# Layer 0's output projection, norm and queries: tile 0 first, tiles 1 to 4 beside its expert pass

## The chip, the cores and the metric

One core of a Trainium2 chip runs the whole program in one launch. The metric is the device time of that launch in microseconds. TensorE (PE) multiplies, VectorE (DVE), ScalarE (ACT) and GpSimd (POOL) work on elements, SyncE (SP) issues transfers, and 16 DMA engines move the bytes. GpSimd issues the indirect transfers (gathers). All data is float32.

## The reference

A two-layer transformer trunk, width 1024, over 512 prompt tokens and 64 sample tokens. In the kernel these are five tiles of 128 rows: 0 to 3 the prompt, 4 the sample (64 rows used). Layer 0 mixes tokens with MLA attention (`o_a`, 512 columns) and an RWKV-7 recurrence (`o_b`, 512 columns); layer 1 with two other mixers. Behind each mixer comes an expert network ("peer"), which picks for every token and each of 8 heads 16 of the rows of two tables:

```python
x = x + jnp.concatenate([o_a, o_b], axis=-1) @ w_out          # even_layer
...
x = x + peer_ffn(rmsnorm(x, norm_ffn), p_wq, p_keys, p_u, p_v)  # run_trunk
...
q = (xb @ w_q).reshape(PEER_BLOCK, PEER_HEADS, 2, half)        # peer_ffn
sc = jnp.einsum('thpd,hpnd->thpn', q, keys)
s1, i1 = lax.top_k(sc[:, :, 0], PEER_TOPK)
s2, i2 = lax.top_k(sc[:, :, 1], PEER_TOPK)
...
top_s, top_pos = lax.top_k(cand, PEER_TOPK)
gate = jax.nn.softmax(top_s, axis=-1)
ue = u_tab[eidx]
ve = v_tab[eidx]
h = jax.nn.gelu(jnp.einsum('td,thkd->thk', xb, ue))
return jnp.einsum('thk,thkd->td', gate * h, ve)
```

## The kernel before

It has stages that follow each other, each a block of its own in which all engines start and end together: norm and input projection of layer 0, `mla`, `rwkv` (two blocks), `project_out`, `norm` with the block `tail`. What the change touches begins at the end of `rwkv`.

`project_out` (L696) fetches the output weights WO as four pieces of 1024 KB (L693) and all X rows again (L147, L148), since X was scratch space in `rwkv`. For each of the five tiles it transposes the attention half OC (L725), copies it to OT, makes two groups of eight products of 128x512 (L738; the RWKV half OBT needs no transpose) and adds them to X on VectorE (L768). `norm` then squares the rows on ScalarE (L184), takes means (L203), the power -0.5 on GpSimd, scales to XN (L210), transposes (L226) and copies to XT (L190), for all five tiles.

The block in `tail` (L2200) makes the expert queries of all tiles first: for each of 8 heads eight products of 512 columns and eight of 64 (L2322), each group copied to QP by ScalarE. `pe_route` multiplies the queries of one tile and head by the keys (L1328), ScalarE copies the scores (L1336), and `dve_route` (from L1355) picks the 16 experts in some 18 steps; its first call runs alone, later ones a step or two at a time between the rows. The first group is routed behind head 0 of the queries, the second behind head 1, yet its scores are copied by ScalarE behind all heads.

The passes run over (layer, tile) in the order 0, 1, 4, 2, 3 in each layer. A pass has 8 heads (4 for tile 4) of 16 slots, 1152 slots in all. In slot s:
- GpSimd gathers, for each of 128 tokens, one row of 8 KB (u and v of the expert, L1434) into place s % 8 of `ring`; it waits until slot s - 8 is used up.
- VectorE makes the dot product of the u half with XN (L1445), ScalarE the gelu and the weight (L1475, L1480).
- TensorE adds the weighted v half in PSUM, by a diagonal that ScalarE builds (L1490) and two products of 128x512 (L1505). In slots that `on_vector` names VectorE does this instead, with one instruction on X (L1455): the first three slots of a pass, and every third, second or fourth slot in the stretches of `SHARES` (L1287).

Layer 1's mixers run beside the slots. A `Layer1` object holds a list of turns for each engine, each with a slot number; `Beside.until` gives an engine's turns when its loop over the slots has come there. The order on an engine is so fixed in the code, and a turn that waits holds up what is behind it. Weights come in slabs of at most 1024 KB, two places in turn, by SP's queue. The first mixer's turns begin at slot 324, the second's at 580; SP runs ahead, and loads the first mixer's gain and first two slabs as soon as the queries are copied.

## Time and profile before

| what | us |
|---|---|
| median of three runs | 3987.99 |
| the three runs | 3987.38, 3987.99, 3992.89 |
| the profiled execution | 3992.78 |
| its span, first to last instruction | 3991.0 |

The rows further down come from the profiled execution. L12 is line 12 of the kernel before. A timeline row gives its start and its length in us, then the engine, the line, the operation, what it writes and reads, and in brackets how long the engine was idle before and what ended that. Of a group of pipelined products the ends are modelled. PEclk is the TensorE clock granted, as a share of full speed. Where a row says SPq, the sequencer of SP issues a transfer.

### The profile page before, as it was taken

To read this page: it belongs to the slowest core of one execution; us is meant where nothing else is said; L and a number is where in the kernel's file an instruction comes from. 1 tells how busy PE (TensorE), PEld (TensorE's weight loads), DVE (VectorE), ACT (ScalarE), POOL (GpSimd) and SP (SyncE) were. 2 spreads that over 40 slices of the span, in tenths; PEclk is the share of its full clock that TensorE was granted. 3 is DMA by queue.
4 is the path that set the end of the run, shared out by engine and by line. 5 is a ranking of instruction groups with operands and counts; after the bars stand their busy time and mean duration, and the time that the engine had idled before them with its cause. 6 is when DMAs were issued, how large, how long until landed. Compare 5 with 4: busy or idle time off the path is not lost.

```text
span 3991.0 us, 34096 instructions
## 1 busy us (share of the span) xinstructions
PE 3176.5 (80%) x9530; PEld 1540.5 (39%) x9530; DVE 2664.8 (67%) x6438; ACT 1344.4 (34%) x3975; POOL 1388.1 (35%) x1218
## 2 busy tenths in 40 slices
PE   7866499787777777779898987888898887776777
PEld 4444389543222332224343442333343422332232
DVE  0087655225667666677999767689977767667664
ACT  1144222012333333333367333333553323333332
POOL 0021000012434444344543444444344444444443
PEclk9987599799999999999999999999899999999999
DMA  3100000237999999999999999999999999999998
GB/s 128 36 1 6 0 1 1 70 122 277 421 421 421 421 418 408 422 404 419 405 384 340 418 386 421 418 420 412 344 417 421 421 402 422 421 421 419 414 416 356
DMA packets 211406, 1284.78 MB, mean 322 GB/s; under 512 B 23568, under 2 KB 38928, under 8 KB 63632
## 3 DMA queue, kind: packets, MB, share of 16 engines
q0 software_dynamic: 165888, 1208.03, 73.9%
q1 hardware_dynamic: 45328, 74.57, 5.3%
q8 instruction: 76, 1.25, 0.1%
q14 instruction: 114, 0.93, 0.1%
HBM read 1278.12 MB, written 3.87 MB: 321 GB/s over the span
## 4 chain that ended last, share of the span: by engine, by line
DMA 37%; PE 20%; DVE 10%; issue 7%; ACT 3%; POOL 2%; DVEq 0%; ACTq 0%; POOLq 0%; SPq 0%
DMA ring<-in_uv,route 36%; PE banks L1505 15%; DVE ring L1445 4%; PE banks L2322 2%; POOL ring L1434 1%; DVE X L1455 1%; ACT route L1490 1%; PE banks L1893 1%; DVE own L2141 1%; ACT route L1475 1%; ACT route L1480 1%; PE banks L1859 0%; PE banks L1833 0%; DMA own<-in_l_peer_wq 0%; DVE QP L2142 0%
## 5 line engine op out<-in xcount | busy, mean ns | idle before, releaser
L1505 PE MATMUL banks<-ring,route 128*128 128x512 f32 (+1 forms) x4224 | 2032.1, 618 | 585.5 <-ACT route L1490 562.4
L1445 DVE SCALAR_TENSOR_TENSOR ring<-ring,XN 128x1024 f32<-128x1024 f32 x1152 | 1409.5, 1224 | 747.7 <-DMA ring<-in_uv,route 739.0
L1434 POOL DMA_INDIRECT ring<-in_uv,route x1152 | 1289.0, 1119 | 1747.0 <-PE banks L1505 1561.9
L1505 PEld LDWEIGHTS banks<-ring,route 128*128 128x128 f32 (+1 forms) x4224 | 745.7, 187 | 1716.4 <-issue 877.3
L1475 ACT ACTIVATE route<-route 128x2 f32<-128x2 f32 x576 | 117.2, 204 | 1837.5 <-DVE ring L1445 1837.1
L1490 ACT ACTIVATE route<-IDN,route 128x128 f32<-128x128 f32 x928 | 318.8, 386 | 1.0 <-PE banks L1505 0.4
L1480 ACT ACTIVATE route<-route 128x1 f32<-128x1 f32 x1152 | 276.7, 287 | 23.2
L1833 PE MATMUL banks<-own,QP 128*128 128x512 f32 (+1 forms) x400 | 177.2, 567 | 4.5 <-DMA own<-in_l_w_in 2.3
L111 POOL TENSOR_TENSOR ys<-ys,IDN 128x4 f32<-128x4 f32 x9 | 9.1, 1008 | 388.6 <-DVE ys L1188 388.6
L1475 ACT ACT_TABLE_LOAD x106 | 136.0, 1283 | 1.9
L1455 DVE SCALAR_TENSOR_TENSOR X<-ring,route,X 128x1024 f32<-128x1024 f32 x96 | 123.0, 1282 | 0.9
L414 PE MATMUL banks<-XT,W 128*128 128x512 f32 (+1 forms) x448 | 121.3, 433 | 0.0
L1833 PEld LDWEIGHTS banks<-own,QP 128*128 128x128 f32 x400 | 76.8, 193 | 93.4 <-issue 82.6
L1445 DVE DVE_READ_ACCUMULATOR ring<-ring,XN 128x1 f32 x1152 | 95.2, 83 | 0.0
L1342 ACT ACT_TABLE_LOAD x72 | 92.4, 1283 | 1.3
L441 DVE COPY SH<-PB 128x14 f32<-128x14 f32 x1 | 0.2, 174 | 137.9 <-ACT PB L430 137.9
L414 PEld LDWEIGHTS banks<-XT,W 128*128 128x128 f32 x448 | 67.7, 191 | 53.9 <-issue 53.9
L1048 PE MATMUL banks<-chunk_more 128*128 128x128 f32 x576 | 78.0, 288 | 12.7 <-DVE chunk_more L1175 4.9
L1048 PEld LDWEIGHTS banks<-chunk_more 128*128 128x128 f32 x576 | 71.6, 200 | 15.9 <-DVE chunk_more L1175 5.8
L1885 PE MATMUL banks<-own,QP 128*128 128x512 f32 x160 | 75.1, 594 | 1.3 <-DMA own<-in_l_w_out 1.2
L1893 PE MATMUL banks<-own 128*128 128x320 f32 (+1 forms) x256 | 71.9, 421 | 5.2 <-DMA own<-in_l_peer_wq 5.2
L1355 DVE MAX8 route<-route 128x8 f32<-128x128 f32 x144 | 34.6, 282 | 55.8 <-ACT route L1336 43.3
(411 smaller groups left out, 3348.3 us busy)
## 6 DMA issues: line engine op xcount, KB each, us to landing
ring<-in_uv,route POOLq DMA_INDIRECT x1152
own<-in_l_w_in SPq DMA_DIRECT2D x16, 1024.0 KB, 16.0
own<-in_l_peer_wq SPq DMA_DIRECT2D x9, 1024.0 KB, 15.9
own<-in_l_w_out SPq DMA_DIRECT2D x8, 1024.0 KB, 16.4
W<-in_l_w_in SPq DMA_DIRECT2D x2, 2560.0 KB, 21.7
X<-in_x_prompt SPq DMA_DIRECT2D x8, 512.0 KB, 8.5
WO<-in_l_w_out SPq DMA_DIRECT2D x4, 1024.0 KB, 9.0
own<-in_l_w_in SPq DMA_DIRECT2D x4, 656.0 KB, 15.8
```

Source lines behind the costliest of these rows:

```text
L414: m = pe.matmul(bank[n % 4][:, 0:b - a], W[:, k, ACOLS + f * P:ACOLS + (f + 1) * P], XT[:, k, a:b], start=(k == 0), stop=(k == KD - 1))
L1048: m = pe.matmul(b[:, p * n:(p + 1) * n], lhs[:, p, :], rhs[:, p, :], start=True, stop=True)
L1342: act.activation(self.GX, self.BS, ACT.Exp, bias=self.NM, accum_out=self.GS[:, 0:1]).then_inc(self.exped.h, 1)
L1434: pool.indirect_dma_start(self.ring[:, s % RING, :], None, self.io[f"uv{of_slot(s)[0]}"], bass.IndirectOffsetOnAxis(ap=self.EI[:, g % 2, k ...
L1445: dve.scalar_tensor_tensor(u, u, 1.0, self.XN[:, of_slot(s)[1], :], ALU.mult, ALU.mult, accum_out=self.HD[:, g % 2, k:k + 1]).then_inc(sel ...
L1455: dve.scalar_tensor_tensor(x, self.ring[:, s % RING, D:], self.WG[:, g % 2, k:k + 1], x, ALU.mult, ALU.add).then_inc(self.v_vector.h, 1)
L1475: act.activation(self.HG[:, par, k:k + 2], self.HD[:, par, k:k + 2], ACT.Gelu).then_inc(self.gelus.h, 1)
L1480: act.activation(self.WG[:, par, k + i:k + i + 1], self.HG[:, par, k + i:k + i + 1], ACT.Copy, scale=self.GT[:, g % 3, k + i:k + i + 1]).t ...
L1490: act.activation(self.DG[:, n % 4, 0:cols], on, ACT.Copy, scale=self.WG[:, par, k + i:k + i + 1]).then_inc(self.diagonals.h, 1)
L1505: m = pe.matmul(self.bank[1 + half][0:n, :], self.DG[:, (V_TENSOR[s] - 1) % 4, 0:n], self.ring[:, s % RING, D + 512 * half:D + 512 * half ...
L1833: m = pe.matmul(out[:, 0:W.shape[2]], self.QP[:, self.tiles[i], k, :], W[:, k % HK, :], start=(k == 0), stop=(k == KD - 1))
L1893: m = pe.matmul(out[:, 0:self.width()], W[:, k % HK, i * P:i * P + P], self.XQ[:, k, 0:self.width()], start=(k == 0), stop=(k == KD - 1))
```

## The change

`project_out`, `norm` for layer 0's experts and their queries are split by tile. The block of `tail` now does output projection, norm and all eight heads of queries for tile 0 alone. A new class `Layer0` does them for tiles 1 to 4 by turns beside the slots of the first pass, as `Layer1` does: output products from slot 9 (one product in 0.71 slots), the norms from slot 48.5, queries from slot 66 to 106. Its weights are fetched a second time, in eight slabs. WO for tile 0 is fetched during the last chunk of `rwkv`, into `ring`; for that `ring` and `own` are allocated from the start, and the stages before use them as scratch in place of buffers of their own. The first six steps of the second group's routing are done ahead of the first dot product. `SHARES` gets the entry (6, 108, 3). VectorE waits for all X rows and the small tables before its first routing, SP loads layer 1's first slabs when `Layer0`'s queries are done.

```diff
-SHARES = [(334, 404, 3), (492, 537, 2), (590, 650, 4), (770, 802, 4), (816, 848, 4)]
+SHARES = [(6, 108, 3), (334, 404, 3), (492, 537, 2), (590, 650, 4), (770, 802, 4), (816, 848, 4)]
...
                 sp.dma_start(ST[:, :, :], io["wkv_t"]).then_inc(loaded.h, 16)
+                wv = io["l0_w_out"].rearrange("(k p) n -> p k n", p=P)
+                for i in (1, 0):
+                    k = slice(4 * i, 4 * i + 4)
+                    sp.dma_start(first_out[:, k, :], wv[:, k, :]).then_inc(wl[i].h, 16)
...
+class Layer0:
...
+        for i in range(4):
+            pe.append((out - 6 + i, "out_turn", i))
+            act.append((out - 4.4 + i, "out_turn", i))
+            for j in range(NO):
+                n = 4 * j + i
+                for k in range(HK):
+                    pe.append((out + (n + k / HK) * o, "out", j // 2, i, HK * (j % 2) + k))
+                if j % 2:
+                    dve.append((out + (n + 1) * o + 1.8, "add", j // 2, i))
+            x = norm + step * i
+            act.append((x, "square", i))
+            dve.append((x + 1, "mean", i))
+            pool.append((x + 1, "root", i))
+            dve.append((x + 3, "scale", i))
+            for b in range(2):
+                pe.append((x + 4 + b, "turn", i, b))
+                act.append((x + 5.6 + b, "xt", i, b))
+        for j in range(NQ):
+            for i in range(4):
+                n = 4 * j + i
+                for k in range(HK):
+                    pe.append((query + (n + k / HK) * q, "query", j // 2, i, HK * (j % 2) + k))
+                if j % 2:
+                    act.append((query + (n + 1) * q + 1.8, "query", 4 * (j // 2) + i))
+        dve.append((query, "zero"))
...
+        for s in range(NO + NQ):
+            if s >= 2:
+                self.slab_end(sp, s - 2)
+            w, c = (w_out, s) if s < NO else (w_q, s - NO)
+            sp.dma_start(self.W[s % 2], w[:, HK * (s % 2):HK * (s % 2) + HK, 512 * (c // 2):512 * (c // 2) + 512]
+                         ).then_inc((self.sl0, self.sl1)[s % 2].h, 16)
...
+            m = pe.matmul(out[:, 0:3 * P + DEC], W[:, k % HK, i * P:i * P + P], self.XQ[:, k, 0:3 * P + DEC],
+                          start=(k == 0), stop=(k == KD - 1))
...
+            sp.dma_start(X[:, 0, :], io["x_prompt"][0, 0:P, :]).then_inc(xl.h, 16)
+            sp.dma_start(rest.GM, io["l0_norm_ffn"].partition_broadcast(P)).then_inc(gl.h, 16)
+            sp.dma_start(WQ, io["l0_peer_wq"].rearrange("(k p) n -> p k n", p=P)).then_inc(wq.h, 16)
             sp.wait_ge(kz.h, kz.at(1))
...
+            for t in range(1, 4):
+                sp.dma_start(X[:, t, :], io["x_prompt"][0, t * P:(t + 1) * P, :]).then_inc(ol.h, 16)
+            sp.dma_start(X[0:DEC, 4, :], io["x_sample"][0]).then_inc(ol.h, 16)
...
-            sp.wait_ge(ev.h, ev.at(QUERIES))
+            rest.sp(sp)
             one.sp(sp)
...
+            for b in range(2):
+                for n, k in enumerate((4, 5, 6, 7, 0, 1, 2, 3)):
+                    if b == 0 and n % 4 == 0:
+                        pe.wait_ge(wo[k // 4].h, wo[k // 4].at(16))
+                    if b == 0 and n == 4:
+                        pe.wait_ge(ot.h, ot.at(1))
+                    lhs = QP[:, 0, k, :] if k < 4 else OBT[:, k - 4, 0:P]
+                    m = pe.matmul(bank[4 + b], lhs, WO[:, k, b * 512:(b + 1) * 512], start=(n == 0), stop=(n == KD - 1))
+                m.then_inc(mm_.h, 1)
...
             for h in range(PH):
...
+                for k in range(KD):
+                    m = pe.matmul(bank[3 + h % 4][:, 0:P], WQ[:, k, h * P:h * P + P], XT0[:, k, :],
+                                  start=(k == 0), stop=(k == KD - 1))
+                m.then_inc(qm.h, 1)
+                if h in (1, 2):
...
+                    ex.pe_route(pe, h - 1)
...
-            dve.wait_ge(ol.h, ol.at(96))
+            dve.wait_ge(ol.h, ol.at(160))
             for _ in ex.dve_route(dve, ch, 0):
                 pass
             route = ex.dve_route(dve, ch, 1)
+            for _ in range(6):
+                next(route)
...
+PLAN_0 = dict(out=9, o=2.85, norm=48.5, step=3, query=66, q=2.5)
```

TensorE from the end of `rwkv` on, before: all transposes and products of project_out, of which the first rows stand here (L725 transposes OC, L738 multiplies by WO), the norm's transposes, and the queries (L2322) with a route product (L1328).

```order
L725 MATMUL banks<-IDN,OC 128x128 x8
L738 MATMUL banks<-WO,OT 128x512 x4
L738 MATMUL banks<-WO,OBT 128x512 x4
L738 MATMUL banks<-WO,OT 128x512 x4
L738 MATMUL banks<-WO,OBT 128x512 x4
L725 MATMUL banks<-IDN,OC 128x128 x4
...
L226 MATMUL banks<-IDN,XN 128x128 x40
...
L2322 MATMUL banks<-own 128x512 x8
L2322 MATMUL banks<-own 128x64 x8
L1328 MATMUL banks<-KY,QP 128x256
```

And now, up to the first weighted row (L1437): L2443 transposes tile 0's OC, L2452 are its output products, L2457 the transposes of XN, L2467 its queries, L2227 the first transpose turn of `Layer0`.

```order
L2443 MATMUL banks<-IDN,own 128x128 x4
L2452 MATMUL banks<-ring,own 128x512 x4
L2452 MATMUL banks<-ring,QP 128x512 x4
L2452 MATMUL banks<-ring,own 128x512 x4
L2452 MATMUL banks<-ring,QP 128x512 x4
L2457 MATMUL banks<-IDN,XN 128x128 x8
L2467 MATMUL banks<-XN,ring 128x128 x16
L1260 MATMUL banks<-KY,QP 128x256
L2467 MATMUL banks<-XN,ring 128x128 x8
L1260 MATMUL banks<-KY,QP 128x256
L2467 MATMUL banks<-XN,ring 128x128 x40
L2227 MATMUL banks<-IDN,own 128x128 x4
```

What moved: 64 output products, 32 transposes and seven eighths of the query work have left the place ahead of the first route.

VectorE in the slots, before, around slot 27: a dot product (L1445) and one routing step in turn.

```order
L1445 SCALAR_TENSOR_TENSOR ring,route<-ring,XN 128x1024
L1365 MAX_INDEX route<-route 128x8
L1366 MAX_INDEX route<-route 128x8
L1445 SCALAR_TENSOR_TENSOR ring,route<-ring,XN 128x1024
L1370 MAX_INDEX route<-route 128x8 x2
L1445 SCALAR_TENSOR_TENSOR ring,route<-ring,XN 128x1024
L1374 CAST route<-route 128x32
```

And now, some slots later, where `Layer0`'s adds (L2300) fall too; L1377 is the dot product, L1387 a row weighed on VectorE.

```order
L1377 SCALAR_TENSOR_TENSOR ring,route<-ring,XN 128x1024
L1387 SCALAR_TENSOR_TENSOR X<-ring,route,X 128x1024
L1330 CAST route<-route 128x32
L1377 SCALAR_TENSOR_TENSOR ring,route<-ring,XN 128x1024
L1333 TENSOR_TENSOR route<-route 128x512
L1377 SCALAR_TENSOR_TENSOR ring,route<-ring,XN 128x1024
L1387 SCALAR_TENSOR_TENSOR X<-ring,route,X 128x1024
L1337 TENSOR_TENSOR route<-route 128x512
L2300 TENSOR_TENSOR X<-banks,X 128x512
```

What moved: one row in three stands on VectorE between the same dot products, and the eight adds with it.

## Rows read from the trace of the kernel before

**Rows 1.** The page: busy time, DMA share and GB/s by slice.
```profile
PE 3176.5 (80%) x9530; PEld 1540.5 (39%) x9530; DVE 2664.8 (67%) x6438; ACT 1344.4 (34%) x3975; POOL 1388.1 (35%) x1218
...
DMA  3100000237999999999999999999999999999998
GB/s 128 36 1 6 0 1 1 70 122 277 421 421 421 421 418 408 422 404 419 405 384 340 418 386 421 418 420 412 344 417 421 421 402 422 421 421 419 414 416 356
```

**Rows 2.** The chain that ended last: by line, then pieces (start us, us, what).
```profile
DMA ring<-in_uv,route 36%; PE banks L1505 15%; DVE ring L1445 4%; PE banks L2322 2%; POOL ring L1434 1%; DVE X L1455 1%; ACT route L1490 1%; PE banks L1893 1%; DVE own L2141 1%; ACT route L1475 1%; ACT route L1480 1%; PE banks L1859 0%; PE 
...
998.77 12.55 DMA ring<-in_uv,route
...
1038.55 12.55 DMA ring<-in_uv,route
```

**Rows 3.** Gathers issued: us, POOL busy (count), PEclk, DMA share, GB/s.
```profile
0.00:1000.00 1000.00, 39.75 (x34) 0.88 0.18 65
998.70:1038.50 39.80, 16.39 (x16) 1.00 1.01 421
```

**Rows 4.** Stretches: us, busy of PE, PEld, DVE, ACT, POOL; PEclk, DMA share, GB/s.
```profile
1000.00:1398.00 398.00, 296.15 (x646) 117.16 (x644) 271.90 (x689) 131.81 (x442) 165.77 (x159) 0.98 1.01 421
1780.00:1930.00 150.00, 138.85 (x334) 63.14 (x332) 115.38 (x269) 42.93 (x138) 75.91 (x57) 0.99 1.02 418
2255.00:2350.00 95.00, 78.10 (x213) 38.94 (x212) 78.54 (x167) 30.30 (x94) 48.77 (x34) 0.95 1.00 399
3035.00:3123.00 88.00, 73.02 (x169) 31.46 (x169) 64.02 (x151) 29.43 (x93) 36.98 (x33) 0.94 1.02 421
```

**Rows 5.** Timeline to the first gather: start us, us, instruction [idle before <-releaser].
```profile
725.18 0.33 SPq L1216 DMA_DIRECT2D STr<-in_wkv_t  x1
...
760.87 1.09 PE L725 MATMUL banks<-IDN,OC 128*128 128x128 f32 x4 [3.04 <-PEq L1205]
...
769.22 6.02 PE L738 MATMUL banks<-WO,OT 128*128 128x512 f32 x8 [5.46 <-DMA WO<-in_l_w_out]
...
775.08 3.60 PE L738 MATMUL banks<-WO,OBT 128*128 128x512 f32 x8
...
781.77 0.69 DVE L768 TENSOR_TENSOR X<-banks,X 128x512 f32<-128x512 f32 x1 [19.76 <-DMA X<-in_x_sample]
...
847.35 1.06 ACT L184 ACTIVATE ring<-X 128x1024 f32<-128x1024 f32 x1 [32.39 <-DMA own<-in_l_norm_ffn]
...
849.78 1.28 DVE L210 SCALAR_TENSOR_TENSOR XN<-X,ssf,own 128x1024 f32<-128x1024 f32 x1
...
853.26 2.19 ACT L190 ACTIVATE own<-banks 128x512 f32<-128x512 f32 x4
...
869.12 0.38 ACT L1336 ACTIVATE route<-banks 128x256 f32<-128x256 f32 x1 [0.85 <-PE banks L1328]
...
871.74 0.49 DVE L1355 MAX8 route<-route 128x8 f32<-128x128 f32 x2 [12.34 <-DMA keep<-in_c_kidx_gain]
...
880.75 1.15 POOL L1434 DMA_INDIRECT ring<-in_uv,route  x1 [8.50 <-DVE route L1414]
```

**Rows 6.** Timeline, first landing to the ninth gather, same columns.
```profile
886.63 1.23 DVE L1445 SCALAR_TENSOR_TENSOR ring<-ring,XN 128x1024 f32<-128x1024 f32 x1 [5.84 <-DMA ring<-in_uv,route]
...
931.13 0.49 DVE L1355 MAX8 route<-route 128x8 f32<-128x128 f32 x2 [43.27 <-ACT route L1336]
...
936.92 1.94 POOL L1434 DMA_INDIRECT ring<-in_uv,route  x1 [45.77 <-DVE X L1455]
```

**Rows 7.** The page: a dot product and a weighted row on VectorE.
```profile
L1445 DVE SCALAR_TENSOR_TENSOR ring<-ring,XN 128x1024 f32<-128x1024 f32 x1152 | 1409.5, 1224 | 747.7 <-DMA ring<-in_uv,route 739.0
...
L1455 DVE SCALAR_TENSOR_TENSOR X<-ring,route,X 128x1024 f32<-128x1024 f32 x96 | 123.0, 1282 | 0.9
```

**Rows 8.** The gather instruction, 1780 to 1930: ns min/median/max, starts.
```profile
L1434 POOL DMA_INDIRECT ring<-in_uv,route x54: 947/1178/2001, 1781.1 to 1928.5; - x54
```

**Rows 9.** The page's DMA issues: 1024 KB slabs, us to landing.
```profile
own<-in_l_w_out SPq DMA_DIRECT2D x8, 1024.0 KB, 16.4
```

466 lines of the change are left out of this document (274 added, 192 removed).

## The prediction

> **What bounds the kernel now.** I read the page first. From 1000 us on nearly every slice moves 400 to 421 GB/s at a DMA share of 9 tenths, while no compute engine is full [rows 1]. The chain that ended last says the same: 36% of the span is the DMA of `ring<-in_uv`, more than anything else [rows 2]. These are the expert gathers: 1152 of them, one 1024 KB gather (1.049 MB) for each (token tile, head, k) slot, in a ring of 8. Two pieces of the chain 16 gathers apart start at 998.77 and 1038.55 [rows 2, 3], so one slot takes 39.78 / 16 = 2.486 us, and 1.049 MB / 2.486 us is the 421 GB/s of [rows 4]. While this holds, only three things move the end: when the stream starts, how many other bytes go through the same DMA engines, and stretches in which an engine holds the ring back.
>
> The stream's start can be given one number. The gather at 998.77 is the 34th (34 are issued before 1000, [rows 3]) and lands at 1011.32. Counting 34 slots back gives 1011.32 - 34 x 2.486 = **926.8** as the effective start. Yet the first gather was issued at 880.75 [rows 5] and landed 5.9 us later, at 886.63 [rows 6]. Had the stream run on from there, its effective start would be 880.75 + 5.9 - 2.5 = 884.15. So 42.65 us are lost after the start: eight gathers fill the ring, then TensorE and ScalarE still work through the queries of all tiles, VectorE waits 43.27 us for the second group's scores in front of its second dot product, and the ninth gather waits 45.77 us for a free slot [rows 6]. Ahead of 880.75, from 760.87 on, stand project_out, norm and the first query for all five tiles, 119.9 us [rows 5]. Only tile 0 is needed for the first 128 slots.
>
> **The change: the head.** I rebuild the path of tile 0 from 760.87, at the durations of [rows 5].
> The output weights (4.2 MB) now are fetched behind the STr load at 725.18, on DMA engines that are nearly idle there (0 to 6 GB/s in the slices from 200 to 700, [rows 1]): at the rate of the X and WO loads below they land in 13 us, over 15 us before their use. So the wait of 5.46 us for WO goes. TensorE: four transposes 1.09 us, then 16 products instead of 80. The granted clock is at its lower level there: of the eight products at 769.22 the group takes 6.02 us, the next eight 3.60 (a pitch of 0.43). I take 6 us for the first eight and 3.5 for the others: 760.9 + 1.1 + 9.5 = 771.5. The two adds of 0.69 lie half beside them: 772.3. Square to scaled row: 849.78 + 1.28 - 847.35 = 3.7 us: 776.0. Eight transposes at the 0.27 of those at 760.87, and the last copy at 2.19 / 4 = 0.55: 3 us: 779. Two heads of queries, 16 products of 128 columns at 0.14 to 0.27 each, a copy, the route product and its copy of 0.38: 4 to 5 us: about 784.
>
> The other condition is new: VectorE waits, ahead of its first routing step, for all X rows and the small tables. Named behind that wait are only this route and all dot products. Ahead in the queue stand X tile 0 and the gain (0.5 MB each), the 4.2 MB query weights, keys 0.6, four X tiles 1.8, tables 0.5: 8.2 MB. Before, WO and X, 6.55 MB, were issued from 760.8 on and had landed at 781.77 [rows 5], 21 us. Scaled by bytes: 26.3 us, so 787. This is later than 784, so the DMA decides; if the scaling applies only to the part above a fixed 2 us it is 786, with the slower of small pieces up to 792.
> Routing before took from 871.74 to the gather at 880.75: 9.0 us. First gather: 787 + 9.0 = **796** (bounds 793 to 803). Effective start 796 + 3.4 = 799.4. The hole of 42.65 us goes too: TensorE has only 6 more heads of tile 0, some 6 to 13 us, in the 9 us of routing and the 5.9 us until the first landing. Gain: 926.8 - 799.4 = **127.4 us**.
>
> **The change: bytes moved into the stream.** WO and the query weights are fetched a second time in eight slabs of 1.049 MB for tiles 1 to 4. The first two need no wait and land between 787 and 796, ahead of the gathers. Six remain, 6.3 MB. Layer 1's gain and first two slabs (0.5 + 2.1 MB), which before lay in the hole after 931, now come after the queries' end, slot 106, and the 0.26 MB copy of sample rows too. Together 9.2 MB at 421 GB/s: **-21.7 us**. Bounds: 20 (part of it in a gap) to 24.
> How good is a count by bytes alone? In 1780 to 1930 the kernel before has the same mix, 1 MB slabs, 1 row in 3 on VectorE, more products than here, and still moves 418 GB/s, 0.7% under 421 [rows 4].
> The Trainium skill, "DMA: Bandwidth & Descriptors", section "Where 436 GB/s comes from", puts the HBM limit of a core at about 358 GB/s. By it this term would be 25.6 us and no slot could take 2.486 us; the rows show 421, so the rows decide.
>
> **The change: work beside the slots.** TensorE gets 16 transposes and 64 products in slots 9 to 55, 32 transposes and 64 products of 448 columns in slots 52 to 106. Per slot it has 2/3 of a row's two products (2 x 0.43, so 0.57) and 1.4 or 1.6 added products at 0.38 to 0.43: 0.6. That is 1.2 of 2.486 us. In 1780 to 1930 it carried more, at a full rate [rows 4]. Slabs: each serves 11.4 (output) or 10 slots (queries), 28 or 25 us, while a slab lands in 16.4 us [rows 9]: hidden.
> VectorE is the tight one. Alone it is busy 271.9 us in 398 us, 160 slots: 1.70 per slot [rows 4]. 34 weighed rows in slots 8 to 107, at 1.28 [rows 7], add 0.43; eight adds of 0.69, four scales of 1.28, the means and a memset add 12 us over 100 slots, 0.12. Sum 2.25 of 2.486, 90%. In the first 20 slots two routing steps go with each dot product, and the need is 2.5 to 2.7: VectorE falls some 3 to 4 us behind, and the ring gives 19.9 us of slack of which a landing takes 12.6 [rows 2]. So I price this by the nearest rows: 0.7% of slots 0 to 107 (267 us) is 1.9; the crowded stretch 2255 to 2350 loses 5%, which would be 13; 3035 to 3123, with the second set's output and norm, loses nothing [rows 4]. Plus 3 us, half of what the restart in the hole cost (936.92 + 3.4 - 8 x 2.486 = 920.4 against 926.8). I take **-5**, bounds 0 and -16.
> What goes from TensorE to VectorE (34 rows, 29 us) gains nothing by itself: neither is late.
> A stall of another kind must be weighed. The gather instruction takes 947 ns at least and 1178 in the median in that stretch [rows 8], and 165.77 / 159 = 1043 in the plain one [rows 4]; 150 us still moved 418 GB/s. The mechanism would be that each added X<-ring,route,X instruction holds Pool back for its length: were all 34 x 1.28 = 43.5 us lost to the stream, that stretch, which has 17 of them by its share of one row in three, would lose 22 of its 150 us, 15%. This is a rule of the Trainium skill, "SBUF — State Buffer" (the part on contention when ops overlap): an instruction of VectorE with two SBUF inputs contends with a GpSimd one that reads SBUF; it leaves open how descriptor writing is hit. By that rule the gather instructions may be longer, and the trace agrees in that; the rate doesn't follow.
>
> **Sum.** 127.4 - 21.7 - 5 = 100.7 us. The profiled execution took 3992.8 (span 3991.0), so 3892.1; the median of the three is 3988.0, 4.8 lower: **3887.3**. The rest of the program is ordered by slots and moves with the stream.
>
> **Rivals.** (1) VectorE is the bound in slots 6 to 107, because in its fixed order it also waits for weights, roots and squares: 2.7 instead of 2.486 us a slot, 22 us more instead of 5: 3904. For it: 90% on paper; against: 77% busy (115.4 of 150) in 1780 to 1930 with no loss. (2) Pool is held back by VectorE as above, 43.5 us: 3988 - (105.7 - 43.5) = 3926. (3) The head is not short: the wait for the X rows and tables lasts longer since the 4 MB of query weights and small pieces lie ahead of them, the first gather at 815: 3906. This is also the case in which the change doesn't do what it says, for tile 0 would wait for the loads of the others. (4) Slower: TensorE stands in order at each slab's first product. That decides if a slab beside the gathers takes over 42 us: six slabs at 50 us against 25 lose 150 us, more than the 105.7, giving 4032. Against it 16.4 us [rows 9]. (5) More than I count: slabs use gaps, no late slots, the first gather at 792: 3876.
>
> **How the numbers follow.** Forecast (3877 to 3899) 0.69; (1) 0.13; (2) 0.04; (3) 0.06; (4) 0.02; (5) 0.04; no net change by something unseen 0.02. The range 3874 to 3914 takes in the forecast, (5), (1) and (3), 0.92 by this list; I keep it since my list may miss things and the bounds of the unknown costs (start 7, VectorE 16, bytes 3 us) make 3880 to 3910 by themselves. Within 0.2% (8 us, about what a measurement of this kernel can tell from no change) 0.01; slower 0.03, faster 0.96.
>
> **What the profile after would show.** First gather at 793 to 803, VectorE's first routing step released by a DMA of `keep`, no wait over 10 us ahead of the ninth gather; from then on 421 GB/s in every slice up to the old place of layer 1, with the 34th gather landing between 885 and 892; gathers in slots 20 to 100 every 2.486 us but for the slabs. Wrong if VectorE shows no idle in slots 6 to 107, if the GB/s there falls under 415, or if TensorE waits for a slab.

## The result, and the profile after

| | before | after |
|---|---|---|
| median, us (range) | 3989.64 (3987.38 to 3992.89) | 3897.65 (3896.55 to 3899.22) |
| ratio after / before | | 0.9769, 95% interval [0.9752, 0.9786] |
| profiled execution, us (span) | 3992.8 (3991.0) | 3896.55 (3894.8) |

The kernel is 92.0 us faster, 2.3%. The forecast was 3887.3, range 3874 to 3914: the time lies in the range, 10.4 us above the forecast. The sum is right to a few us, but two of the terms in it rest on a wrong count, and one sentence was wrong outright.

The page after, its lines on busy time, DMA share and GB/s (beside [rows 1]) and its two costliest lines of gathers and weighed rows (beside [rows 7]):
```profile
PE 3111.6 (80%) x9394; PEld 1521.5 (39%) x9394; DVE 2702.3 (69%) x6472; ACT 1335.9 (34%) x3949; POOL 1427.4 (37%) x1217
...
DMA  3100000399999999999989999999999999999998
GB/s 131 34 4 7 0 1 1 118 366 418 416 419 419 420 414 411 415 412 417 392 339 394 396 387 420 419 416 407 354 419 421 421 409 422 421 420 413 415 420 354
...
L1366 POOL DMA_INDIRECT ring<-in_uv,route x1152 | 1330.3, 1155 | 1684.1 <-PE banks L1437 1497.5
...
L1387 DVE SCALAR_TENSOR_TENSOR X<-ring,route,X 128x1024 f32<-128x1024 f32 x130 | 166.5, 1281 | 0.9
```
A slice is 97 us. The ninth to eleventh slices of [rows 1] moved 122, 277 and 421 GB/s; now they move 366, 418 and 416: the stream starts a slice earlier, and its hole is gone. The later slices look as before.

The timeline after, from the start of the last block to the first gather and the ninth (start us, us, instruction, idle before and its releaser), beside [rows 5]. The first line is the block's start, which was at 760.87:
```profile
758.16 1.09 PE L2443 MATMUL banks<-IDN,own 128*128 128x128 f32 x4 [3.04 <-PEq L1133]
...
759.03 4.58 PE L2452 MATMUL banks<-ring,own 128*128 128x512 f32 x8
...
763.45 3.60 PE L2452 MATMUL banks<-ring,QP 128*128 128x512 f32 x8
...
766.88 3.60 PE L2452 MATMUL banks<-ring,own 128*128 128x512 f32 x8
...
770.31 3.60 PE L2452 MATMUL banks<-ring,QP 128*128 128x512 f32 x8
...
778.10 1.97 PE L2457 MATMUL banks<-IDN,XN 128*128 128x128 f32 x8 [4.19 <-DVE XN L2548]
...
780.80 5.76 PE L2467 MATMUL banks<-XN,ring 128*128 128x128 f32 x32 [0.73 <-issue]
...
785.87 0.64 POOL L2428 TENSOR_SCALAR_AFFINE_SELECT keep<-keep 128x512 f32<-128x512 f32 x1 [9.22 <-DMA keep<-in_c_kidx_gain]
...
786.39 0.60 PE L1260 MATMUL banks<-KY,QP 128*128 128x256 f32 x2
...
787.54 0.49 DVE L1287 MAX8 route<-route 128x8 f32<-128x128 f32 x2 [9.50 <-ACT route L1268]
...
797.19 1.15 POOL L1366 DMA_INDIRECT ring<-in_uv,route  x1 [10.68 <-DVE route L1346]
...
811.36 1.94 POOL L1366 DMA_INDIRECT ring<-in_uv,route  x1 [4.28 <-DVE X L1387]
```
The reader is to see three things. The four groups of L2452 hold 32 matmul records for 16 products in the code: a product of f32 with 512 columns is **two records of 0.43 us**, 0.86 us, once the clock is full. VectorE's first routing step (L1287) is released by ScalarE's copy of the scores, not by a DMA; Pool's affine step, which waits for the same loads, shows that they had landed at 785.87, 1.7 us earlier. And from the block's start to the first gather it is 39.03 us, where it was 880.75 - 760.87 = 119.88.

Stretches after (us; busy of PE, PEld, DVE, ACT, POOL; PEclk, DMA share, GB/s). The first holds the added output products, the second the added queries; columns as in [rows 4]:
```profile
826.00:940.00 114.00, 103.16 (x236) 44.38 (x235) 92.65 (x212) 34.45 (x109) 53.81 (x45) 0.99 1.02 419
1000.00:1080.00 80.00, 74.05 (x181) 33.94 (x180) 60.90 (x134) 25.70 (x85) 39.84 (x30) 0.98 1.02 419
```
TensorE is busy 103.16 of 114 us in the first, VectorE 92.65. The tight engine is TensorE.

**Where the 96.2 us between the two profiled executions are.** The trace's packets date the landing of every gather, and what the other queues moved between two landings. Of each stretch of slots I take the time less 2.486 us a slot, and of that the bytes of the other queues at 421 GB/s:

| | predicted, us | from the packets, us |
|---|---|---|
| effective start of the stream | +127.4 | +124.8 |
| bytes moved into slots 0 to 128 | -21.7 | -22.2 |
| other loss in slots 0 to 128 | -5 | -2.7 |
| slots 128 to 192 | 0 | -1.1 |
| slots 496 to 560 (layer 1, first mixer's output stage) | 0 | -5.1 |
| the rest | 0 | +2.8 |
| sum | 100.7 | 96.5 |

The parts are good to about half a us each, so the sum misses the 96.2 us by 0.3. A landing here is the end of a gather's last packet.

### The profile page after: what moved, and what is told of

It is laid out like the page before. It is cut to its first block, busy times and chain, and to the rows that moved or that the text cites. A ratio compares the mean times of both kernels' runs of the same rounds, so it can differ in the third digit from the quotient of the medians.

```text
span 3894.8 us, 33849 instructions
## 1 busy us (share of the span) xinstructions
PE 3111.6 (80%) x9394; PEld 1521.5 (39%) x9394; DVE 2702.3 (69%) x6472; ACT 1335.9 (34%) x3949; POOL 1427.4 (37%) x1217
## 4 chain that ended last, share of the span: by engine, by line
DMA 39%; PE 20%; DVE 10%; issue 7%; ACT 3%; POOL 1%; DVEq 0%; ACTq 0%; POOLq 0%
DMA ring<-in_uv,route 38%; PE banks L1437 14%; DVE ring L1377 4%; DVE X L1387 1%; PE banks L1765 1%; ACT route L1422 1%; POOL ring L1366 1%; PE banks L1825 1%; DVE own L2073 1%; PE banks L1817 1%; ACT route L1407 1%; ACT route L1412 1%; PE banks L1791 1%; DMA own<-in_l_w_out 0%; DMA own<-in_l_peer_wq 0%
## 5 line engine op out<-in xcount | busy, mean ns | idle before, releaser
L1437 PE MATMUL banks<-ring,route 128*128 128x512 f32 (+1 forms) x4088 | 1980.6, 621 | 564.1 <-ACT route L1422 547.1
L1366 POOL DMA_INDIRECT ring<-in_uv,route x1152 | 1330.3, 1155 | 1684.1 <-PE banks L1437 1497.5
L1377 DVE SCALAR_TENSOR_TENSOR ring<-ring,XN 128x1024 f32<-128x1024 f32 x1152 | 1409.7, 1224 | 726.6 <-DMA ring<-in_uv,route 718.1
L1437 PEld LDWEIGHTS banks<-ring,route 128*128 128x128 f32 (+1 forms) x4088 | 723.8, 188 | 1650.7 <-issue 831.3
L1422 ACT ACTIVATE route<-IDN,route 128x128 f32<-128x128 f32 x894 | 309.5, 387 | 4.0 <-PE banks L1437 2.8
L1387 DVE SCALAR_TENSOR_TENSOR X<-ring,route,X 128x1024 f32<-128x1024 f32 x130 | 166.5, 1281 | 0.9
L111 POOL TENSOR_TENSOR ys<-ys,IDN 128x4 f32<-128x4 f32 x9 | 9.1, 1009 | 388.6 <-DVE ys L1114 388.6
L1377 DVE DVE_READ_ACCUMULATOR ring<-ring,XN 128x1 f32 x1152 | 95.6, 83 | 0.0
L440 PE MATMUL banks<-XT,ring 128*128 128x512 f32 (+1 forms) x320 | 86.6, 433 | 0.0
L440 PEld LDWEIGHTS banks<-XT,ring 128*128 128x128 f32 x320 | 48.4, 191 | 38.6 <-issue 38.6
L1825 PEld LDWEIGHTS banks<-own 128*128 128x128 f32 x256 | 47.4, 190 | 39.7 <-issue 24.9
L974 PE MATMUL banks<-chunk_more 128*128 128x128 f32 x360 | 49.6, 289 | 7.5 <-DVE chunk_more L1091 3.0
```

What stands on the lines that cost most here:

```text
L440: m = pe.matmul(bank[n % 4][:, 0:b - a], W[1 + f // 5][:, k, f % 5 * P:(f % 5 + 1) * P], XT[:, k, a:b], start=(k == 0), stop=(k == KD - 1))
L1366: pool.indirect_dma_start(self.ring[:, s % RING, :], None, self.io[f"uv{of_slot(s)[0]}"], bass.IndirectOffsetOnAxis(ap=self.EI[:, g % 2, k ...
L1377: dve.scalar_tensor_tensor(u, u, 1.0, self.XN[:, of_slot(s)[1], :], ALU.mult, ALU.mult, accum_out=self.HD[:, g % 2, k:k + 1]).then_inc(sel ...
L1387: dve.scalar_tensor_tensor(x, self.ring[:, s % RING, D:], self.WG[:, g % 2, k:k + 1], x, ALU.mult, ALU.add).then_inc(self.v_vector.h, 1)
L1422: act.activation(self.DG[:, n % 4, 0:cols], on, ACT.Copy, scale=self.WG[:, par, k + i:k + i + 1]).then_inc(self.diagonals.h, 1)
L1437: m = pe.matmul(self.bank[1 + half][0:n, :], self.DG[:, (V_TENSOR[s] - 1) % 4, 0:n], self.ring[:, s % RING, D + 512 * half:D + 512 * half ...
```

## The experiments

Before each quoted expectation stands its edit; medians are beside the changed kernel's 3897.65, ratios are to the kernel before, with 95% intervals. The kernels ran in four groups, each beside the kernel before, whose median there was 3989.88 (no_share, share2, before_share, quarter_slabs), 3988.55 (wo_late, obt_early, route_early, both_early), 3990.77 (share4, split_early, after_again) and 3990.14 (split_share4). A difference in us between two groups is uncertain by these 2 us; the ratios are not.

**Does the sharing of rows gain anything?** Three kernels change one entry of SHARES. The first takes it out:
```diff
-SHARES = [(6, 108, 3), (334, 404, 3), ...
+SHARES = [(334, 404, 3), ...
```


> The changed kernel (3897.65 us) without its entry (6, 108, 3) in SHARES: no row in slots 6 to 107 goes to VectorE. The prediction said that this entry gains nothing by itself: 3897 +- 3. My theory after the trace: a product of 128x128 by 128x512 is two matmul records of 0.43, not one, so TensorE needs 1.72 us for a row and 1.2 more for the added products, 2.92 us a slot where a slot lasts 2.486: 20 us later over slots 9 to 55, up to 17 over 66 to 106, less what the ring and the pause between them absorb: 3920 to 3934, and no idle time of TensorE there. If instead the X instructions of VectorE hold the gather instructions back, it is 5 to 40 us faster, and the gathers' mean falls from 1155 to about 1119 ns in both cases.


Measured: 3911.33 (3906.44 to 3911.73), ratio 0.9804 [0.9788, 0.982], 13.7 us over the changed kernel. The same stretches as above, of this kernel:
```profile
826.00:940.00 114.00, 114.00 (x277) 51.54 (x276) 73.70 (x192) 37.40 (x121) 46.11 (x40) 1.00 1.01 405
1000.00:1080.00 80.00, 79.14 (x198) 37.13 (x197) 50.36 (x129) 27.72 (x92) 34.11 (x27) 1.00 1.01 411
```
TensorE doesn't rest for 114 us, and the stream falls to 405 GB/s: 40 gathers are issued where the changed kernel issues 45. By the packets slots 32 to 112 take 16.2 us more. The prediction's "gains nothing by itself" is refuted, TensorE as the bound is shown. The size was less than I expected, 13.7 instead of 20 to 37: the ring lets TensorE fall some 7 us behind (19.9 us of ring less a landing of 12.6) once in each of the two crowded stretches, and my sum of 20 + 17 had not taken that off in numbers; that account is argued, not tested. The gather instructions take 1133 ns in the mean of all 1152, between the 1155 and the 1119 expected. That is weak evidence on what lengthens them (share2, with 17 more rows on VectorE, has 1155 too); before_share below shows it.

The second shares more:
```diff
-SHARES = [(6, 108, 3), (334, 404, 3), ...
+SHARES = [(6, 108, 2), (334, 404, 3), ...
```


> The changed kernel with one row in two on VectorE in slots 6 to 107 instead of one in three. VectorE would need 1.70 + 0.64 + 0.12 = 2.46 of 2.486 us a slot, TensorE 0.86 + 1.2 = 2.06. If VectorE is the tight one, as the prediction had it, 3905 to 3915; if it has room beyond the count, the same as the changed kernel within 2 us.


Measured: 3901.05 (3896.38 to 3902.69), ratio 0.9778 [0.9762, 0.9795]. It can't be told from the changed kernel. VectorE at a counted 2.46 of 2.486 us a slot is not late: its rate stays at 418 GB/s between 860 and 940, with VectorE busy 68.67 of 80 us. The count for VectorE was too high, which is seen below too. Where it really becomes the bound no run shows.

The third shares less:
```diff
-SHARES = [(6, 108, 3), (334, 404, 3), ...
+SHARES = [(6, 108, 4), (334, 404, 3), ...
```


> The changed kernel with one row in four on VectorE in slots 6 to 107. By the corrected count TensorE needs 0.75 x 1.72 + 1.2 = 2.49 us a slot, just what a slot lasts (2.486), and VectorE 2.14. If TensorE's records of 0.43 us are its whole cost, within 3 us of the changed kernel; if its cost per slot is higher than the count (as no_share would have it if all its loss came from one rate), 5 to 10 us slower. With all rows on TensorE it was 13.7 us slower, with one in two 3.4 (inside the spread).


Measured: 3895.36 (3893.71 to 3897.08), ratio 0.9762 [0.9748, 0.9777]. By the packets slots 32 to 96 lose 4.8 us beyond their bytes, where the two profiles of the changed kernel lose 2.1 and 3.9: the place itself gained nothing. The profiled execution is 1.7 us shorter than the changed kernel's, and its block began 2.8 us earlier (755.41), which is enough for that. Between one row in two and one in four no difference in the time is seen; only without the sharing TensorE is late.

**Does VectorE's X instruction hold Pool back?** The kernel before, with the entry alone:
```diff
-SHARES = [(334, 404, 3), (492, 537, 2), ...
+SHARES = [(6, 108, 3), (334, 404, 3), (492, 537, 2), ...
```


> The kernel before (3989.64 us) with the entry (6, 108, 3) in SHARES alone: one row in three to VectorE where nothing stands beside the slots. TensorE needs 1.72 of 2.486 us a slot there, so neither engine is late: within 2 us of the kernel before. If VectorE's X instructions held Pool back by their length, 34 x 1.28 = 43.5 us slower; the gather instructions' mean in this stretch then shows by how much it is longer without any slab or product beside it.


Measured: 3989.92 (3985.76 to 3995.24), ratio 1.0002 [0.9992, 1.0012]. Of the kernel before, the group of gather instructions between 1000 and 1180 (count, busy us, mean ns, idle before and its releasers):
```profile
L1434 POOL DMA_INDIRECT ring<-in_uv,route x72 | 72.7, 1009 | 105.8 <-PE banks L1505 104.9 <-issue 0.9
```
Its stretch (columns as above):
```profile
1000.00:1180.00 180.00, 136.01 (x301) 53.88 (x300) 121.48 (x310) 61.84 (x205) 72.66 (x72) 1.00 1.01 421
```
Of this kernel, the same group:
```profile
L1434 POOL DMA_INDIRECT ring<-in_uv,route x72 | 93.7, 1302 | 86.5 <-PE banks L1505 67.2 <-DVE X L1455 10.2 <-issue 9.1
```
And the stretch:
```profile
1000.00:1180.00 180.00, 117.39 (x199) 43.90 (x197) 147.48 (x331) 55.74 (x180) 93.56 (x72) 0.82 1.01 421
```
The gather instruction grows from 1009 to 1302 ns, 21 us in 72 gathers, and the stream moves 421 GB/s and 72 gathers in both. Pool still has 86.5 us of idle time in 180, so the lengthening is paid from idle time. The second rival (43.5 us lost) is refuted.

What lengthens a gather instruction can be read from the starts and ends of all 72 in each kernel. In this kernel 51 of them start while one of VectorE's two long instructions (dot product or X instruction, 1.2 to 1.3 us) is under way, in the kernel before 4. Such a gather instruction ends 0.81 us after that instruction does (median; 0.810 to 0.815 for most); one that starts at another time takes 0.94 us (median in both kernels). One of each:
```profile
1034.17 1.23 DVE L1445 SCALAR_TENSOR_TENSOR ring<-ring,XN 128x1024 f32<-128x1024 f32 x1 [0.59 <-DMA ring<-in_uv,route]
...
1034.35 1.86 POOL L1434 DMA_INDIRECT ring<-in_uv,route  x1 [0.30 <-issue]
...
1038.39 0.94 POOL L1434 DMA_INDIRECT ring<-in_uv,route  x1 [2.17 <-PE banks L1505]
...
1039.17 1.23 DVE L1445 SCALAR_TENSOR_TENSOR ring<-ring,XN 128x1024 f32<-128x1024 f32 x1 [1.11 <-DMA ring<-in_uv,route]
```
The first started 0.18 us into a dot product, the second 0.78 us ahead of one, and neither dot product is longer for it. Of the 51, 46 met a dot product and only 5 an X instruction. So the X instruction doesn't mainly hold Pool back for its own length: with it in the order, gathers start at other times against the dot products. Why they do is open. The rule that the prediction weighed beside it, of the Trainium skill, "SBUF — State Buffer", section "SBUF: two separate sides" (a VectorE instruction with two SBUF inputs and a GpSimd one that reads SBUF exclude each other, whichever starts first), agrees with this in both directions; that the wait costs the stream nothing while Pool has slack is what the rows add.

**Do the moved bytes cost their time?** This kernel leaves three quarters of the third to the eighth slab unfetched, so tiles 1 to 4 get other values and the instructions stay the same.
```diff
-            sp.dma_start(self.W[s % 2], w[:, HK * (s % 2):HK * (s % 2) + HK, ...
+            n = HK if s < 2 else 1
+            sp.dma_start(self.W[s % 2][:, 0:n, :], w[:, HK * (s % 2):HK * (s % 2) + n, ...
```


> The changed kernel, in which the third to the eighth slab of layer 0's weights for tiles 1 to 4 fetch only one row in four (the rest of the slab keeps the numbers of an earlier one, so the products of those tiles are not the reference's; everything else is done as before). 4.72 MB less on the DMA engines: if the moved bytes cost what they take at 421 GB/s, 11.2 us faster, 3886.5. If slabs use gaps, less; if waits of TensorE for slabs or a clash of slabs and gathers cost more than the bytes, more.


Measured: 3889.46 (3881.49 to 3891.41), 8.2 us under the changed kernel where 11.2 were expected. By the packets slots 16 to 96 take 9.0 us less with 4.7 MB less than in the first profile of the changed kernel, and 10.7 less than in its second (after_again below). So seven tenths of the bytes' time to nearly all of it comes back, and no more than it: slabs don't use gaps to any large part, and no wait for a slab costs more than its bytes. The intervals of the two ratios overlap, so the packets carry this reading and the medians only agree with it. Whether one or two of the 11 us really stay is open; TensorE is busy 94.22 of 100 us between 980 and 1080 in this kernel, so it may be what the stream meets next.

**What decides the first gather, the loads or the compute?** Four kernels. In the first the output weights come late:
```diff
 (block before)
-                for i in (1, 0):
-                    k = slice(4 * i, 4 * i + 4)
-                    sp.dma_start(first_out[:, k, :], wv[:, k, :]).then_inc(wl[i].h, 16)
 (last block, sync, at its start)
+            for i in (1, 0):
+                k = slice(4 * i, 4 * i + 4)
+                sp.dma_start(WO[:, k, :], wv[:, k, :]).then_inc(wo[i].h, 16)
```


> The changed kernel, in which the 4.2 MB of layer 0's output weights are fetched at the start of the last block, ahead of the X tile 0, and no longer in the block before. Two things get worse: the first products wait 5.5 us for the weights, as in the kernel before; and the other loads, behind 4.2 MB more, land 10.5 us later, so the wait for X rows and tables (met at 785.9 in the changed kernel, 1.6 us before the compute path asks) would come at 796 and decide. If the DMA queue decides once it is longer: +8 to +10 us, with VectorE's first routing step released by a DMA. If only the compute path counts: +5.5.


Measured: 3908.64 (3904.51 to 3910.36), ratio 0.9798 [0.9783, 0.9813], 11.0 us over the changed kernel. Its timeline (block start 759.29):
```profile
768.01 5.45 PE L2452 MATMUL banks<-ring,own 128*128 128x512 f32 x8 [7.63 <-DMA ring<-in_l_w_out]
...
799.09 0.49 DVE L1283 MAX8 route<-route 128x8 f32<-128x128 f32 x2 [11.19 <-DMA keep<-in_c_kidx_gain]
```
The weights cost 7.63 us of wait, and then the loads behind them decide: they land 39.8 us after the block's start instead of 27.7, and VectorE's first routing step is released by that DMA. The expected +8 to +10 was 1 to 3 us low; 4.2 MB more took 12.1 us on this queue and not 10.5, which is 1.6 of them. The DMA condition of the prediction is real; it is only not the later one in the changed kernel.

The second shortens the compute path alone:
```diff
 (block before, tensor)
                 for c, k in turns:
                     pe_stage(pe, c, k)
+                    if (c, k) in ((last, 15), (last, 17)):
+                        if k == 15:
+                            pe.wait_ge(wl[1].h, wl[1].at(16))
+                        half = (k - 15) // 2
+                        for q in range(4):
+                            pe.matmul(bank[6 + half], OBT[:, q, 0:P],
+                                      first_out[:, 4 + q, half * 512:half * 512 + 512], start=(q == 0), stop=False)
 (last block, tensor: the other eight products go on in banks 6 and 7)
-                for n, k in enumerate((4, 5, 6, 7, 0, 1, 2, 3)):
+                for k in range(4):
```


> An attempt to beat the changed kernel. The head of its last block has 16 products for tile 0 that take 32 matmul records (15 us), all in one row; eight of them need only the second mixer's output, done long ago, and weights that land near 735. They are moved into two idle stretches of TensorE in the block before (from 747.6 to 753.2, and after 755.1), in two banks that nothing uses there. My theory (the head is a chain of compute, TensorE first in it): 5 to 7 us faster. Rival (the wait for the X rows and tables decides the first gather, as the prediction said): no more than 1.5 us faster, since these land at 785.9 whatever the products do.


Measured: 3899.04 (3896.29 to 3899.72), ratio 0.9777 [0.9762, 0.9792]. No gain in the median. Its timeline, the copy of the scores and then the first routing step (block start 759.88):
```profile
783.61 0.38 ACT L1275 ACTIVATE route<-banks 128x256 f32<-128x256 f32 x1 [0.16 <-PE banks L1267]
...
787.12 0.49 DVE L1294 MAX8 route<-route 128x8 f32<-128x128 f32 x2 [14.59 <-DMA keep<-in_c_kidx_gain]
```
The scores were there at 784.0, and VectorE then stood until 787.12 for the X rows and tables. The mechanism of the rival is shown: with the compute path shortened, the prediction's condition decides. The first gather comes 36.90 us after the block's start, 2.1 to 4.2 us sooner than in the two profiles of the changed kernel; some 0.7 us go back to a later block start, since the moved products now end last in the block before (TensorE until 759.6). The rest is as large as the spread of the medians, and doesn't show in them.

Moving the products did a second thing. The 16 records left in the last block take 7.11 us, all at 0.43, and the granted clock is 1.00 from 751.7 to 772.2: TensorE worked up to the block's end, and the block starts at the full clock. In the changed kernel TensorE rests 3.04 us ahead of the block, starts it at the lower clock, and its first eight records alone take 4.58 to 6.16 us (below). So part of the shorter head, here and in the faster kernels further down, is clock and not a shorter list of products: an estimated 1.0 to 2.6 us, the 4.58 to 6.16 less the 3.60 of later groups.

The third takes the wait away and reorders two steps:
```diff
 (tensor)
-                if h in (1, 2):
-                    if h == 1:
-                        pe.wait_ge(kl.h, kl.at(64))
-                    pe.wait_ge(ev.h, ev.at(h))
-                    ex.pe_route(pe, h - 1)
+                if h == 0:
+                    pe.wait_ge(kl.h, kl.at(64))
+                if h in (0, 2):
+                    pe.wait_ge(ev.h, ev.at(max(h, 1)))
+                    ex.pe_route(pe, h // 2)
 (scalar)
-                if h == 1:
+                if h == 0:
                     ex.act_copy(act, 0)
 (vector)
-            dve.wait_ge(ol.h, ol.at(160))
             for _ in ex.dve_route(dve, ch, 0):
                 pass
+            dve.wait_ge(ol.h, ol.at(160))
```


> The changed kernel with the key scores of tile 0's first head directly behind that head's query (before, the second head's query stood between), and VectorE's wait for the X rows and tables behind the first routing instead of ahead of it. 1.5 to 2.5 us faster, of which the wait alone gives nothing in the changed kernel. Too small to be told in the median; the trace must show the first routing step 1.5 to 2.5 us closer to the block's start.


Measured: 3898.75 (3895.69 to 3903.05), ratio 0.9775 [0.976, 0.979]. No change in the median, and the trace doesn't show the step earlier than in the changed kernel's first profile (30.06 against 29.38 us after the block's start). The table below says why: that first profile had the shortest head of all with this code. Against the second profile (31.46) it is 1.4 us earlier, and against all five others with this head (30.79 to 31.74) 0.7 to 1.7, so at best the lower end of what was expected. The expectation was set against an outlier.

The fourth has both edits.


> Both together. The wait for the X rows and tables would become the last condition of the shorter head if it stayed where it was; moved behind the first routing it is out of the way. By the compute chain: 7 to 9 us faster than the changed kernel, 3889 to 3891. If something else decides (the landing of query weights or keys, near 780 to 783): 4 to 6.


Measured: 3889.85 (3887.04 to 3894.8), ratio 0.9756 [0.9742, 0.9769], 7.8 us under the changed kernel. The first routing step is 22.1 us after the block's start, ahead of the landing at 27.6: with the wait out of the way the shorter compute path counts in full: the first gather is 32.07 us after the block's start, 7.0 to 9.0 less than in the changed kernel's two profiles. (The two ratios' intervals overlap; the head is the clearer evidence.) In its timeline TensorE now waits for the next load:
```profile
773.84 3.56 PE L2472 MATMUL banks<-XN,ring 128*128 128x128 f32 x16 [2.69 <-DMA ring<-in_l_peer_wq]
```

**A faster kernel.** To both edits come the transposes of OC in the block before, and the query weights in two pieces:
```diff
 (block before: tensor; scalar copies bank 7 back to OC[:, 0, :])
+                    if (c, k) == (last - 1, 17):
+                        for q in range(4):
+                            m = pe.transpose(bank[7][:, q * P:(q + 1) * P], OC[:, 0, q * P:(q + 1) * P], ident)
+                        m.then_inc(oct_.h, 1)
 (last block, sync)
-            sp.dma_start(WQ, io["l0_peer_wq"].rearrange("(k p) n -> p k n", p=P)).then_inc(wq.h, 16)
+            sp.dma_start(WQ[:, :, 0:2 * P], wqv[:, :, 0:2 * P]).then_inc(wq.h, 16)
             ...
             keys(0)
+            sp.dma_start(WQ[:, :, 2 * P:], wqv[:, :, 2 * P:]).then_inc(wq2.h, 16)
```


> Both_early (3889.85 us) and two things more: tile 0's transposes of the first mixer's output go to an idle stretch of TensorE in the block before, with their copy, so that the last block starts with products (1.4 us); and the query weights come in two pieces, the two heads that the first routings need ahead of the keys, so that TensorE doesn't wait 2.7 us for 4.2 MB. First gather 28 to 29.5 us after the block's start instead of 32.1; 2.5 to 4 us faster than both_early, 3886 to 3887.5. If something else decides there, the first routing step stays at 22.1 us after the block's start.


Measured: **3884.16** (3882.75 to 3888.19), ratio 0.9735 [0.9721, 0.9748]: 13.5 us under the changed kernel, 106 us under the kernel before. The first gather is 29.71 us after the block's start:
```profile
756.11 7.10 PE L2464 MATMUL banks<-ring,own 128*128 128x512 f32 x16 [0.30 <-PEq L1133]
...
784.00 0.64 POOL L2446 TENSOR_SCALAR_AFFINE_SELECT keep<-keep 128x512 f32<-128x512 f32 x1 [18.05 <-DMA keep<-in_c_kidx_gain]
...
785.82 1.15 POOL L1381 DMA_INDIRECT ring<-in_uv,route  x1 [1.17 <-DVE route L1361]
```
That is a little more than the 28 to 29.5 expected; the median is 5.7 us under both_early where 2.5 to 4 were expected, 2 of them uncertain since the two belong to different groups. Against the changed kernel in its own group (after_again, 3900.32) it is 16.2 us faster. Pool's own wait for the tables ends 1.2 us before the gather, so after about one more microsecond saved on the compute path the loads would decide.

Then the same with one row in four, `(6, 108, 4)`:


> Split_early (3884.16 us) with one row in four on VectorE in slots 6 to 107. If the 2.3 to 5 us by which share4 lay under the changed kernel belong to the sharing, 3879 to 3882; if they were the difference of block starts and of chips (its block began at 755.4, 2.8 us before that of the changed kernel), 3884 +- 2 again. Its loss in slots 32 to 96 beyond the bytes was 2.7 us higher than the changed kernel's, so I expect the second.


Measured: 3885.44 (3883.79 to 3889.28), ratio 0.9742 [0.9729, 0.9756]. The second case: the sharing makes no difference there either.

**How far a profile repeats.** The changed kernel once more, in five runs:


> The changed kernel itself, beside the others on one chip, to see how far its profile repeats: block start 758 +- 3 us, first gather 39 to 40 us after it, median 3897.5 +- 1. If the 5 us that slots 496 to 560 lost more than in the kernel before belong to the change, they are there again (37 us over 2.486 us a slot, of them 23.4 bytes); if not, 32 to 34.


Measured: 3900.32 (3897.67 to 3902.68), ratio 0.9774 [0.976, 0.9787]; the median of all nine runs of it is 3898.28. The median and the first gather (41.11) miss their expected ranges by 1.8 and 1.1 us: the first profile and the first median were both on the short side. The profile says more than the median:

| kernel | block start, us | first gather after it, us |
|---|---|---|
| before | 760.87 | 119.88 |
| before_share | 756.82 | 121.19 |
| after | 758.16 | 39.03 |
| after_again | 760.59 | 41.11 |
| no_share, share2, share4 | 758.61, 760.23, 755.41 | 41.39, 40.44, 41.23 |
| quarter_slabs | 754.99 | 41.23 |
| wo_late | 759.29 | 49.45 |
| obt_early, route_early | 759.88, 757.27 | 36.90, 39.71 |
| both_early | 756.94 | 32.07 |
| split_early, split_share4 | 756.11, 754.70 | 29.71, 29.91 |

Up to the block's start the changed kernels differ in nothing, in a few instructions or (wo_late) in one load, and yet it lies anywhere between 754.7 and 760.6; the two with the old head have 756.8 and 760.9. So the 2.7 us between the two profiles first compared can't be called a gain of the change. With the 5.1 us of slots 496 to 560 it is less clear. They take 37.3 us over 2.486 us a slot in the first profile of the changed kernel, 35.2 in its second, 32.1 in the kernel before, 33.2 in before_share, and 33.5 to 38.6 in the others, which all share its code there. Profiles of nearly the same code differ by 5 us here, but all twelve with the change lie above both without it, 35.5 in the mean against 32.7. So some 3 us may belong to the change after all. I expected 37 or 32 to 34 and got a number between; what makes this stretch vary, and what the change could do to it, is open.

The head itself varies by TensorE's clock. The granted clock went from the lower level (1.2 GHz) to the full one (2.4 GHz) at 760.99 in the first profile, 2.8 us after the block's start, and at 766.23 in the second, 5.6 us after it. The first group of L2452 took 4.58 us in the first profile and 5.97 in the second:
```profile
761.47 5.97 PE L2452 MATMUL banks<-ring,own 128*128 128x512 f32 x8
```
The group of the queries, ahead of which the clock had fallen back, took 5.76 and 6.43 us. Together this is the 2.1 us between 39.03 and 41.11.

## Why the prediction was right, and where not

**The bound and the start.** That from the first landing on one gather takes 2.486 us, and that the gain is the earlier start, held: 124.8 us by the packets against 127.4. The first gather was 1.2 us late; most of the rest is that the prediction dated the 34th landing before at 1011.32, where the packets' count has 1009.1. The hole of 42.65 us went as foreseen: the ninth gather waited 4.28 us, not 45.77 [rows 6], and the 34th gather had landed at 889.9 by its completion signals (887.5 by the packets' count), within the 885 to 892 named.

**The head.** First gather forecast at 796, measured 797.19. The closeness is partly luck. From the block's start it is 35.1 us by the prediction, 39.03 in this profile and about 41 in the other five profiles with this head. The failed step is the one on the products: "16 products instead of 80 ... I take 6 us for the first eight and 3.5 for the others ... 9.5". The x8 in [rows 5] counts matmul records, and eight records are four products; the list of TensorE's instructions under "The change" has the same groups as x4. The 16 products took 14.9 us (759.03 to 773.9), 5.4 more; with slower queries the compute path was ready 29.4 us after the block's start and not 23.1. A block start 2.7 us earlier hid most of it. The loads landed 27.7 us after the start where scaling by bytes gave 26.1. So "the DMA decides" was wrong in this kernel, by 1.7 us, and right as soon as the compute path was shortened (obt_early) or the queue lengthened (wo_late). The Trainium skill, "FP8 and Floating Point Precision", section "TensorE Precision Notes", counts four passes through the array for true FP32. The trace agrees in so far as a product takes more than one record; how four passes would lie in two records no run here shows. Read beforehand, it would have been a reason to count the records of a product.

**The bytes.** 21.7 predicted, 22.2 by the packets, and quarter_slabs returned 8.2 to 10.7 of an expected 11.2. The term stands.

**The work beside the slots.** The sum (-5, measured -2.7) was right for a wrong reason. TensorE's need was put at 1.2 us a slot, from products at 0.43. At two records a product it is 2/3 of 1.72 for the rows and 1.4 x 0.86 for the added products, 2.35; the stretch above shows 103.16 / 45 = 2.29. [rows 4] held this already: 296.15 us of TensorE in 160 slots, 4.04 records and 1.85 us a slot, in a stretch with nothing beside the rows. VectorE's need was taken from that row, TensorE's was not. VectorE was put at 2.25 and was at 92.65 / 45 = 2.06. So the sentence "gains nothing by itself: neither is late" is the outright error: without the sharing the kernel is 13.7 us slower (no_share). Its half about the kernel before is right (before_share: 1.0002).

**The rivals.** (1), VectorE as bound: refuted by share2, which gives it 17 more rows for nothing that can be measured. A rival with TensorE in its place would have been the right one to list. (2) refuted by before_share: the gather instruction is longer, but mostly by dot products that it meets, and the stream loses nothing. (3), late loads at 815: they landed at 785.87. (4), TensorE standing at each slab: not seen. (5), more gain: not seen.

**From the profiled sum to the median.** The profiled gain is 96.2 us where 100.7 were predicted, 4.5 short. The prediction then took 4.8 us off, by which the profiled execution of before lay over its median, as if this held after too; the profiled execution after lies 1.1 us under its median. 4.5 + 4.8 + 1.1 = 10.4 us, the whole difference.

## What to carry to other kernels

Take each engine's need per step from a busy time divided by a count of steps, for all engines alike; a product in the code may be two records in the trace, and a duration read beside "x8" is of records. Where two conditions for one step lie within a few us of each other, price both: shortening the later one alone gains no more than their distance (obt_early and route_early alone nothing that the medians show, both 7.8, split_early 13.5 us). And before a difference of 3 to 5 us in some far stretch is explained, profile the same kernel again: here the last block's start varied by 6 us among kernels that are nearly the same up to there, and one stretch of 64 slots by 5.

## What the runs showed of the hardware

- The gather instruction on Pool grew from 1009 to 1302 ns in the mean when VectorE took one row in three beside it (before and before_share, 1000 to 1180). A gather instruction that starts while a VectorE instruction with two inputs in SBUF (1.2 to 1.3 us) is under way ends 0.81 us after that one ends, 51 of 72 against 4 of 72; the others take 0.94 us, and VectorE's are not longer. The stream stayed at 421 GB/s: 29% more on an engine that still had 86.5 of 180 us idle cost nothing.
- In the same stretch TensorE's granted clock fell from 1.00 to 0.82, a mean between its full level of 2.4 GHz and its lower one of 1.2, as its busy time fell from 136 to 117 of 180 us. In that kernel, taking rows away from TensorE lowered its clock, and it cost nothing; in the changed kernel, where the added products fill the place of the rows, it stayed at 0.98 to 0.99.
- TensorE's clock in the head of the block differs between executions of the same code: the first eight records of 512 columns took 4.58 to 6.16 us there, behind 3.04 us without work, and whole groups of eight behind them 3.60. With work up to 0.30 us before the block (obt_early, both_early, split_early) the first sixteen took 7.10 to 7.11, at a granted clock of 1.00.
